# Two groups of tokens or three in the first layer of a hybrid SSD, RG-LRU and PEER trunk on one NeuronCore

## The reference

```python
def layer(x, c, ...):
    sh1, sc1, g1, sh2, sc2, g2 = split(silu(c) @ w_mod + b_mod, 6)
    h = rmsnorm(x, ln1_w) * (1.0 + sc1) + sh1
    proj = h @ w_in              # z, xbc, dt, lx, ly, g_ssd, g_lru
    # xbc: causal conv (4 wide), silu, SSD scan with 16 heads x 64; y * silu(z), rmsnorm
    # lx:  causal conv, RG-LRU scan over time; times gelu(ly)
    merged = sigmoid(g_ssd) * (y_ssd @ w_br_ssd) + sigmoid(g_lru) * (y_lru @ w_br_lru)
    x = x + g1 * (merged @ w_out)
    h = rmsnorm(x, ln2_w) * (1.0 + sc2) + sh2
    return x + g2 * peer(h)
def peer(h):                     # 8 heads, each the best 16 of 128 x 128 product keys
    # per token 128 experts e with gates g:  sum_k gelu(h . u[e_k]) * g_k * v[e_k]
```

## Time and profile before

| | us |
|---|---|
| median of 3 runs (4737.82 to 4742.53) | 4742.3 |
| the profiled execution | 4738.38 |
| its span | 4736.6 |
| PE busy | 3245.1 (69%) |
| DVE busy | 3076.3 (65%) |
| POOL busy | 1425.4 (30%) |
| ACT busy | 1159.3 (24%) |
| first gather issued at | 711.1 |
| DMA traffic | 1610.78 MB, of which 1342.26 MB are gathers |

### The profile page before, as it was taken

How to read it: one execution, slowest core, us unless ns; L and a number is a source line. 1 busy time by engine, 2 the same in 40 slices (tenths; PEclk the granted TensorE clock), 3 DMA queues, 4 the chain that set the end, 5 groups by cost and what they waited for, 6 DMA issues and landing times. The chain is left out here.

```text
span 4736.6 us, 59682 instructions
## 1 busy us (share of the span) xinstructions
PE 3245.1 (69%) x21986; PEld 1908.1 (40%) x21986; DVE 3076.3 (65%) x8034; ACT 1159.3 (24%) x3203; POOL 1425.4 (30%) x1298
## 2 busy tenths in 40 slices
PE   7899984677677764489999764677677664444443
PEld 4455552445455442144455431445455442112111
DVE  2443067885864587687854696976964588685554
ACT  2123012332421222223521222232521222122111
POOL 0000003323233334322332324333333334444442
PEclk8999996778788776589999876778788876556555
DMA  8333328989999999968999978989999999999998
GB/s 323 141 135 110 98 72 339 366 316 355 373 401 412 419 383 371 400 258 320 360 371 366 353 281 356 370 323 411 390 415 409 419 394 364 421 421 405 421 421 342
DMA packets 279855, 1610.78 MB, mean 340 GB/s; under 512 B 56411, under 2 KB 61329, under 8 KB 112525
## 3 DMA queue, kind: packets, MB, share of 16 engines
q0 software_dynamic: 184320, 1342.26, 70.4%
q1 hardware_dynamic: 65808, 255.49, 14.5%
q10 hardware_dynamic: 29436, 9.24, 0.8%
HBM read 1597.63 MB, written 7.91 MB: 339 GB/s over the span
## 5 line engine op out<-in xcount | busy, mean ns | idle before, releaser
L527 POOL DMA_INDIRECT ring<-in_peer_uv,units x1280 | 1422.2, 1111 | 3276.6 <-PE psum L922 2347.8
L1810 DVE SCALAR_TENSOR_TENSOR ring<-ring,hrow 128x1024 f32<-128x1024 f32 x1280 | 1544.9, 1223 | 810.7 <-DMA ring<-in_peer_uv,units 796.9
L922 PE MATMUL psum<-ring,diag 128*32 128x256 f32 x10240 | 938.2, 498 | 1222.5 <-ACT diag L1255 1209.7
L540 PE MATMUL psum<-hT,wslot 128*128 128x384 f32 (+1 forms) x4224 | 1286.4, 462 | 17.6 <-issue 8.0
L922 PEld LDWEIGHTS psum<-ring,diag 128*32 128x32 f32 x10240 | 325.3, 132 | 1752.5 <-ACT diag L1255 1435.5
L540 PEld LDWEIGHTS psum<-hT,wslot 128*128 128x128 f32 x4224 | 848.1, 205 | 448.7 <-issue 108.5
L1296 ACT ACTIVATE gel<-hid 128x2 f32<-128x2 f32 x640 | 129.3, 202 | 1631.4 <-DVE ring L1810 1599.9
L1255 ACT ACTIVATE diag<-pick,wgt 128x32 f32<-128x32 f32 x1280 | 338.7, 312 | 736.5 <-DVE wgt L1818 627.6
L540 PE MATMUL psum<-region,wslot 128*128 128x384 f32 (+1 forms) x1536 | 451.8, 450 | 13.6 <-DVE region L1650 9.2
L540 PEld LDWEIGHTS psum<-region,wslot 128*128 128x128 f32 x1536 | 297.9, 198 | 161.5 <-issue 24.8
L1818 DVE TENSOR_TENSOR wgt<-gel,units 128x2 f32<-128x2 f32 x640 | 100.5, 157 | 160.6 <-ACT gel L1296 150.6
(11 more groups left out here) (250 smaller groups left out, 2933.3 us busy)
## 6 DMA issues: line engine op xcount, KB each, us to landing
wslot<-in_w_tiles SPq DMA_DIRECT2D x360, 512.0 KB
ring<-in_w_modt SPq DMA_DIRECT2D x24, 2048.0 KB, 8.9
ring<-in_peer_uv,units POOLq DMA_INDIRECT x1280
wslot<-in_w_gate SPq DMA_DIRECT2D x32, 128.0 KB
region<-in_states_t SPq DMA_DIRECT2D x16, 256.0 KB
region<-in_states_n SPq DMA_DIRECT2D x16, 256.0 KB
out_new_ssd_sample<-region ACTq DMA_DIRECT2D x16, 256.0 KB
xT<-in_x_t SPq DMA_DIRECT2D x1, 2560.0 KB, 8.9
```

Of the source, the lines that this page charges most:

```text
L527: pool.indirect_dma_start(ring[:, n, :], None, table, bass.IndirectOffsetOnAxis(ap=units[:, s % 2, block, 0, quad:quad + 1].bitcast(U32), ...
L540: last = pe.matmul(out, wslot[:, n % SLOTS, k * P:(k + 1) * P], src(k), start=k == 0, stop=k == KT - 1)
L922: last = pe.matmul(psum[c * BLOCK:(c + 1) * BLOCK, block % 2, block // 2 * 256:(block // 2 + 1) * 256], diag[:, n, :], ring[:, n, D + c * ...
L1810: dve.scalar_tensor_tensor(out=ring[:, n, 0:D], in0=ring[:, n, 0:D], scalar=1.0, in1=hrow[:, e % 2, :], op0=ALU.mult, op1=ALU.mult, accum_ ...
```

## The change

The list of groups becomes a list for each layer. The first layer has three groups: tiles 0 and 1, tile 2, and tiles 3 and 4; the second keeps its two. So there are 5 regions, of 256, 128, 256, 384 and 256 tokens. Region 0's SSD stage has 13 steps in place of 19, region 1's has 7, and that of a region with the streams 16 in place of 15. Counted over all pairs, region 1 now lies at pairs 16 to 79, region 2 at 81 to 184, region 3 (the former 2) at 200 to 316, region 4 (the former 3) at 328 to 507. Pairs 0 to 15 lie beside the last 8 steps of region 0 as before.

```diff
-FIRST, COUNT = (0, 3), (3, 2)
-T0 = (0, 3 * P)
-NG = (3 * P, 2 * P)
-PN = (3 * P, P)
-REGIONS = 2 * DEPTH
+GROUPS = (((0, 2), (2, 1), (3, 2)), ((0, 3), (3, 2)))
+REGION = [(l, *group) for l in range(DEPTH) for group in GROUPS[l]]
+REGIONS = len(REGION)
+LAYER, FIRST, COUNT = zip(*REGION)
...
-    b["Z"] = b["S"] + (19 if g == 0 else 15)
+    b["Z"] = b["S"] + 6 * COUNT[r] + (4 if r in ENDS else 1)
...
-SHARE = {"N1": 4, "X": 14, "S": 10, "Z": 18, "LX": 17, "LRU": 25, "M": 17, "OUT": 10, "Q": 24}
+SHARE = {"N1": 3, "X": 12, "S": 9, "Z": 12, "LX": 12, "LRU": 20, "M": 12, "OUT": 7, "Q": 22}
...
+SPANS = (None, (16, 80), (81, 185), (200, 317), (328, 509))
...
-    window(fresh + pairs_of(1, 2), steps_of(1), 0, 64 - 28 + 125)
-    window(pairs_of(3, 4), steps_of(2), 9, 122)
-    window(pairs_of(5, 6, 7), steps_of(3), 9, 180)
+    queue = fresh + pairs_of(*range(1, 8))
+    begun = PAIRS - len(fresh)
+    for r in range(1, REGIONS):
+        until = (SPANS[r + 1][0] if r + 1 < REGIONS else 8 * PAIRS) - begun
+        window(queue[:until], steps_of(r), SPANS[r][0] - begun, SPANS[r][1] - begun)
+        queue, begun = queue[until:], begun + until
```

```diff
+def state_slot(i):
+    return i % 2 if i < 8 else (i - 8) % 3
...
-                        slot = i % 5
-                        if i >= 5:
-                            if i - 5 < 8:
-                                sp.wait_ge(S["yoff"], at("yoff", l, i - 5))
-                            else:
-                                sp.wait_ge(state_out[slot], 16 * state_stores(l, i - 13))
+                        slot = state_slot(i)
+                        if 2 <= i < 10:
+                            sp.wait_ge(S["yoff"], at("yoff", l, i - 2))
+                        elif i == 10:
+                            sp.wait_ge(S["dec"], l + 1)
+                        elif i > 10:
+                            sp.wait_ge(state_out[slot], 16 * state_stores(l, i - 11))
...
-                if self.sample:
-                    self.states = room(at + 5504, 5, 512)
-                    self.tail_rows = room(27 * N, 7, 512)
+                self.xw = room(at + (2048 if low else 4480), HEADS, HD)
+                if self.sample:
+                    self.states = (room(at + 5504, 512), room(at + 6016, 512), room(at + 1536, 512))
+                    self.tail_rows = room((22 if low else 27) * N, 3, 512)
```

More of the change, by code:

```diff
@@ L68, in bases @@
     return b
-BASE = [bases(r % 2) for r in range(REGIONS)]
+BASE = [bases(r) for r in range(REGIONS)]
 LENGTH = [BASE[r]["END"] for r in range(REGIONS)]
@@ L181, in same_group @@
 def same_group(s):
-    return s % NT not in (2, 4)
+    return s + 1 < TILES_E and s + 1 not in STARTS
 def within(s):
@@ L214, in spreads @@
     return BLOCKS * BLOCKS * (s + 2)
+def state_slot(i):
+    return i % 2 if i < 8 else (i - 8) % 3
 def state_loads(l, i):
-    return sum(1 for u in range(DEPTH) for v in range(16) if (u, v) <= (l, i) and v % 5 == i % 5)
+    return sum(1 for u in range(DEPTH) for v in range(16) if (u, v) <= (l, i) and state_slot(v) == state_slot(i))
 def state_stores(l, j):
-    return sum(1 for u in range(DEPTH) for v in range(8) if (u, v) <= (l, j) and (8 + v) % 5 == (8 + j) % 5)
+    return sum(1 for u in range(DEPTH) for v in range(8) if (u, v) <= (l, j) and v % 3 == j % 3)
 def chosen(r):
-    return PH * sum(COUNT[u % 2] for u in range(r))
+    return PH * sum(COUNT[0:r])
 def build(nc, a):
@@ L243, in build @@
         mod_in = [sem(f"mod_in_{s}") for s in range(4)]
-        state_in = [sem(f"state_in_{s}") for s in range(5)]
-        state_out = [sem(f"state_out_{s}") for s in range(5)]
+        state_in = [sem(f"state_in_{s}") for s in range(3)]
+        state_out = [sem(f"state_out_{s}") for s in range(3)]
         written = sem("written")
@@ L380, in __init__ @@
                 self.lacc = room(24 * N + 2 * (self.pad + 1), self.pad + 1)
-                self.lru = [room(18 * N + i * N, N) for i in range(9 if g else 8)]
+                self.lru = [room(18 * N + i * N, N) for i in range(8)]
                 self.rec = room(26 * N, N)
@@ L386, in streams @@
                 return v[:, HIST + self.PN:self.pad].rearrange("p (b t) -> p b t", b=STREAMS)
-        G = (Layout(0), Layout(1))
+        G = [Layout(r) for r in range(REGIONS)]
         cin = room(0, KT, 9)
-        def mod_row(c):
-            return room(RM - 512 if c < 12 else 8 * NG[0], 512)
+        mod_row = room(RM - 512, 512)
         mod_slab = ring[:].rearrange("p n c -> p (n c)").rearrange("p (s c) -> p s c", s=4)
@@ L732, in ssd_stage @@
                 def ssd_stage(r, i):
[L733 removed]
+                    for u in range(COUNT[r]):
                         ssd_tile(r, u, i - 6 * u)
                 def z_stage(r, i):
[L737 to L738 removed]
+                    lay = G[r]
+                    l = lay.l
                     if 0 <= i < 8:
@@ L951, in turn_h @@
                     pe.wait_ge(E["h_rows"], 2 + turned["h"])
-                    if t in FIRST and block == 0 and s and half == 0:
-                        r = 2 * l + FIRST.index(t)
+                    if s in STARTS and block == 0 and s and half == 0:
+                        r = STARTS[s]
                         pe.wait_ge(S["modulated"], at("modulated", 2 * r + 1, 7))
-                        if G[r % 2].sample:
+                        if G[r].sample:
                             pe.wait_ge(S["sampled"], at("sampled", l, 1))
@@ L1026, in fill @@
                         act.wait_ge(S["conved"], at("conved", r, j - 2))
+                    if not lay.first:
+                        act.activation(x[:, 0:HIST], carry[:, j, :], ACT.Copy)
                     if not lay.sample:
@@ L1328, in _ @@
                 act.wait_ge(written, WRITTEN + 16 * NT)
-                for slot in range(5):
-                    act.wait_ge(state_out[slot], 16 * sum(1 for l in range(DEPTH) for j in range(8) if (8 + j) % 5 == slot))
+                for slot in range(3):
+                    act.wait_ge(state_out[slot], 16 * state_stores(DEPTH - 1, 6 + slot if slot < 2 else 5))
             @block.vector
@@ L1444, in x_stage @@
                 def x_stage(r, i):
-                    l, g = divmod(r, 2)
-                    lay = G[g]
+                    lay = G[r]
+                    l = lay.l
                     n = lay.nt * HEADS
                     v = dt[:, 0:lay.nt, :].rearrange("p t h -> p (t h)")
-                    if i == 0 and not lay.sample:
+                    if i == 0 and lay.first:
                         dve.memset(lay.xpad[:, :, 0:HIST], 0.0).then_inc(S["zeroed"], 1)
@@ L1488, in ssd_tile @@
                             dve.wait_ge(S["silued"], at("silued", r, 9))
-                            if r == 2:
+                            if l and lay.first:
                                 dve.wait_ge(written, 256)
@@ L1584, in lx_stage @@
                 def lx_stage(r, i):
-                    lay = G[r % 2]
-                    if i == 0 and not lay.sample:
+                    lay = G[r]
+                    if i == 0 and lay.first:
                         dve.memset(lay.lpad[:, :, 0:HIST], 0.0).then_inc(S["zeroed"], 1)
```

268 lines of the change are left out of this document (139 added, 129 removed).

## The result

The changed kernel takes 4756.87 us (median of 7 runs, 4750.59 to 4766.35), the kernel before in the same rounds 4742.53. The ratio is 1.0031, 95% interval 1.0021 to 1.0042: slower by 0.3%. The forecast was 4724, faster; the time lies in the range (4640 to 4810), the direction was wrong. Over the rounds of the experiments the median of the kernel before lay between 4734.7 and 4742.5 us, so runs of different rounds are compared by their ratios to it.

A forecast was written before the change was run, and what follows sets the result against it. It took PE to bound until the first gather, then the gathers' bytes plus what dense windows lose: 4738 - 161 - 12 + 149 + 20 - 10 = 4724 us, range 4640 to 4810.

The forecast's parts named there:

- region 0 to the first pair: Region 0 with 256 tokens for 384: 161 us less, first gather near 550 us in place of 711.
- pairs 0 to 15: Pairs beside region 0's last four heads: four best_keys less, 12 us saved.
- pairs 16 to 184: Regions 1 and 2 beside 169 pairs: 149 us more for dense windows, plus 10 for states.
- from pair 185 on: Layer two: 10 us saved beside the 384-token region, 10 lost to the state slots.
- The dense windows: Regions 1 and 2: 1.09 and 1.07 of byte time, means of DVE-based and PE-based factors, 497 + 735 us, +149.
- the rival for slower: Regions 1 and 2: chains of short waits set the pace; decides from factor 1.10, sum 4749 us; chance 0.33.
- Second layer: 384-token region of layer two: four more pairs beside it cost less than alone, -10 us; last region 0.
- Three slots for the states: State updates: store and load round trips stall, mostly covered; 10 us for each of two regions, 20 in all.

The follow-up runs named there:

- e1: Changed kernel with the states in five slots again, waits and steps as in the kernel before: 0.9991 of the kernel before, 4734.6 us.
- e4: Changed kernel, region 1 loading only 128 of the 1024 columns of each weight tile, every instruction kept: 0.9959 of the kernel before.
- e12: Changed kernel with five slots, the second part of the choice left out for tile 2 in region 1's Q: 0.9939 of the kernel before, 4708.0 us.
- e6: Changed kernel with two groups in layer one, of two and three tiles, so no third pass over the weights: 1.0031 of the kernel before.
- e3: Changed kernel with five slots and layer two's old spans and shares: 0.9996 of the kernel before, 4735.3 us.
- e2: Changed kernel, three slots kept, with layer two's old spans and shares: 1.0028 of the kernel before.
- e7: Kernel before (old groups, shares and spans) with the three state slots, three tail buffers and their waits: 1.0044 of the kernel before.
- e5: Changed kernel with ACT's wait for the last state stores moved from before LX to where the memory is written: 1.0028 of the kernel before.
- e9: Changed kernel, three slots, SP loading the last three state blocks after the fifth, sixth and seventh Z tile: 1.0030 of the kernel before.
- e15: Changed kernel with five slots and, in regions 1 to 4, fewer pairs beside M, more beside LX, LRU and Q: 1.0016 of the kernel before.

## Why the prediction was wrong

By its own sum, trace against trace, -14 us were forecast and +15 measured:

| step | forecast | measured |
|---|---|---|
| region 0 to the first pair | -161 | -166 |
| pairs 0 to 15 | -12 | -8 |
| pairs 16 to 184, with 10 for the states there | +159 | +168 |
| from pair 185 on, with 10 for the states there | 0 | +22 |

- **Region 0** was right, in the stages read. DVE's first instruction of LRU comes 70 us earlier, for a forecast of 65. From M's first update on DVE to OUT's first it took 108.3 us in place of 159.8, so 51 for 54; LRU 48 in place of 55, so 7. The pace of a product, 0.12 us at 128 columns and half of what 256 cost, held in region 1 (16 in 2.02 us, 0.11 from start to start):

```profile
864.04 2.02 PE L563 MATMUL psum<-region,wslot 128*128 128x128 f32 x16 [1.08 <-DMA wslot<-in_w_tiles]
```

- **The dense windows failed in size**, and most of the error is theirs: "I take the means, 1.09 and 1.07". With the slots out of the way (e1) region 1 takes 506 us for its 64 pairs and region 2 750 for the next 105, so 1.11 and 1.09 of the byte time, +170 where 149 were forecast. That is the point from which the rival for slower was to decide (1.10). A part is a misreading: on a line between the old windows (78 and 87%) a DVE share of 82% says 1.13 and not 1.11, and the means were rounded down; without that the sum has some 9 us more, and still says faster.
- **What the factor hides.** Laid out by stage, the changed kernel's region 1 loses its DMA time in four places: some 20 us in Q (DMA share 0.86), 13 in S (0.61), 9 in N1 and X (0.85), 6 in LRU (0.89), and nothing in Z, LX, M and OUT (1.01 and 1.02). e4 shows that bytes do not set the pace in these four, e12 that DVE's work does in Q. In LRU DVE is busy 91%. In X and S no engine is full (DVE 73 and 79%, PE 72 and 70%), nor is one in e6; that its chains of short waits set the pace there, as the rival had it, is argued from that and not shown by a run. The changed kernel's N1 and X, then S:

```profile
647.00:704.00 57.00, 40.90 (x411) 33.19 (x403) 41.46 (x129) 21.68 (x76) 18.92 (x17) 0.89 0.85 334
704.00:737.00 33.00, 22.97 (x142) 12.36 (x143) 26.07 (x53) 11.80 (x23) 7.74 (x6) 0.69 0.61 239
```

  Even the slowest engine of each stage, added up (bytes at 400 GB/s, PE, DVE or ACT), gives only 469 of the 505 us: a sum of busy times, by region or by stage, is a floor here.
- **"Second layer"**, put at -10, failed too: more pairs beside the 384-token region are worth nothing that can be told (e3 and e1 do not differ, nor e2 and the changed kernel), and e1's layer two stands at +1 (-4.9 at pair 200, -3.8 at the end). It was one more mean: that region has DMA shares of 0.74 to 0.81 in its X, S and Q stages, and, as I read it, the new shares do not put the four pairs to use there.
- **"Three slots for the states"**: 20 us in all were forecast, 19 are measured (e1 against the changed kernel; 21 in e7). The sum was met with some luck, for the place was wrong. I put 10 us on each layer. In region 4, where DMA share is 1.01 without the stall, nearly all of it is lost. In layer one the changed kernel and e1 are 3 us apart after pair 185, the other way; the four traces with three slots and this plan (changed, e2, e5, e9) stand at -7 to +4 there, those with five (e1, e3) at -4 and -1, so some 2 us at most. The waits of DVE came as forecast in number in region 2, three, but shorter (14.4 us in all, 8 each forecast), and in region 4, where the loss is, they are 7.1 us in two, hardly more than the 5.6 of e1 (13 to 15 in e2, e5 and e7). That is why layer two stands at +22.
- So of 29 us between forecast and trace, 21 are the dense windows', 11 the second layer's plan, and the rest (-3) small. Without the slots the kernel would have been 4 us faster than before (e1, just clear of nothing), not 34.
- The Trainium skill (DMA: Bandwidth & Descriptors, on the fixed cost: 2.0 us and the bytes, fitted for DMAs issued from GpSimd) would have the slots cost nothing, by the estimate in the prediction. e1 and e7 speak against it here, with 19 and 21 us; they do not say how long a round trip takes.

What is open: along which waits the slots' cost reaches the gathers of region 4; the split between four and five slots (above); what sets the pace in X and S; and why region 2 hides the stall, which is argued from its DMA share (0.94), and from e7, which stands 6 us behind at pair 80 and 2 at pair 185.

## What to carry to other kernels

A stall that prefetch seems to cover was free here only where the DMA engines had idle time to catch up (share 0.94); where their share is 1.0, cost it in full. When work runs beside a bandwidth-bound stream, read the DMA share stage by stage. The stages with a share of 1.0 and those below it want different amounts of the stream's work: moving it from M (1.02) to LX, LRU and Q (0.86) gave 17 us here, the new grouping 4 before that and 16 with it, while the same shares in layer two, where PE is full in M of region 3, cost 28 (e15). And do not cost such a window by a mean of busy times: dense work displaced beside the stream took back all of 170 us, and even the busiest engine of each stage, added up, left 36 of region 1's 505 us out. The measured loss of the nearest stages is the better guide.

## What the hardware showed that I had not expected

- Issuing the store of one 256 KB block mostly took ACT's queue 0.4 us, but in these two kernels up to 13 when another had been issued a microsecond before (13.1 us in region 4 of the changed kernel, 13.0 in region 1 of the kernel before).
- A 128-column product that loads new weights starts 0.11 us after the one before it at 2.4 GHz (granted clock 0.98 in M of region 1), against 0.216 and 0.322 us for 256 and 384 columns. It is then at a floor: in the kernel before, 8 products with 9 columns and new 128-column weights each take 0.95 us, and the last of them 0.26 by itself, so they too start 0.11 us apart.

```profile
209.49 0.95 PE L579 MATMUL psum<-pick,region 128*128 128x9 f32 x8
```
